# Padding the rows of the moving operands, and eight start residues for the weight slots

## What is computed

```
x = x + 0.5 * swiglu(rmsnorm(x, ffn1_norm[l]), w_ffn1_in[l], w_ffn1_out[l])
u = rmsnorm(x, mix_norm[l])
... = split_sizes(u @ w_in[l], IN_SPLITS)
...
x = x + merged @ w_out[l]
x = x + 0.5 * swiglu(rmsnorm(x, ffn2_norm[l]), w_ffn2_in[l], w_ffn2_out[l])
```

## Time and profile before

| | |
|---|---|
| time, median of 3 runs | 2471.56 us |
| time of the profiled execution | 2470.84 us |
| span of the profiled execution | 2469.0 us |
| TensorE matmul busy | 2440.9 us (99%), 20,948 matmul records |
| TensorE weight load busy | 2380.7 us (96%) |
| VectorE busy | 1673.3 us (68%) |
| ScalarE busy | 1279.0 us (52%) |
| GpSimd busy | 404.8 us (16%) |
| moved by DMA | 410.11 MB, mean 166 GB/s |
| granted TensorE clock, mean | 0.996 of full speed |

### The profile page before, as it was taken

The page is one execution under the profiler, slowest core; times in us unless marked ns, Lnnn a source line. Parts: engine busy times, 40 slices in busy tenths (PEclk is TensorE's granted clock), DMA queues, the critical chain, the costliest instruction groups (busy, mean ns, idle before and its releaser), DMA issues.

```text
span 2469.0 us, 49272 instructions
## 1 busy us (share of the span) xinstructions
PE 2440.9 (99%) x20948; PEld 2380.7 (96%) x20948; DVE 1673.3 (68%) x2315; ACT 1279.0 (52%) x1812; POOL 404.8 (16%) x357
## 2 busy tenths in 40 slices
PE   8999999999999999999999999999999999999998
PEld 8999999999999999999999999989999999999998
DVE  7765776866667657878666766866666665866664
ACT  5544656644445456565454544745444444754443
POOL 4012110300200210203003013512002003422001
PEclk9999999999999999999999999999999999999999
DMA  6555433455555544345555555403555555402553
GB/s 241 188 188 180 162 124 133 173 188 186 188 188 188 188 171 154 120 139 195 185 190 191 205 203 183 155 19 120 186 185 179 187 189 186 161 26 98 193 188 120
DMA packets 57675, 410.11 MB, mean 166 GB/s; under 512 B 6384, under 2 KB 6640, under 8 KB 8688
## 3 DMA queue, kind: packets, MB, share of 16 engines
q1 hardware_dynamic: 56592, 402.15, 45.9%
q10 hardware_dynamic: 864, 4.82, 0.5%
HBM read 405.89 MB, written 1.05 MB: 165 GB/s over the span
## 4 chain that ended last, share of the span: by engine, by line
PE 87%; DVE 5%; ACT 3%; issue 3%; POOL 2%; DMA 0%; DVEq 0%; SPq 0%; POOLq 0%; ACTq 0%
PE bank L297 86%; DVE sb_wlo L310 2%; ACT area L306 2%; DVE area L310 2%; DVE area L321 1%; PE bank L301 1%; ACT sb_whi L306 1%; POOL area L310 0%; ACT L306 0%; POOL sb_x_ssq L310 0%; POOL area L315 0%; POOL sb_x_sq L310 0%; DVE sb_x L321 0%; DMA sb_x<-x 0%; POOL area L334 0%
## 5 line engine op out<-in xcount | busy, mean ns | idle before, releaser
L297 PE MATMUL bank<-area,sb_whi 128*128 128x256 f32 x11752 | 2093.6, 281 | 11.0 <-DVE area L321 5.7
L297 PEld LDWEIGHTS bank<-area,sb_whi 128*128 128x128 f32 x11752 | 1799.7, 188 | 23.8 <-DVE area L321 9.6
L297 PE MATMUL bank<-area,sb_wlo 128*128 128x256 f32 x5876 | 1642.3, 279 | 4.5 <-DVE sb_wlo L310 4.4
L306 ACT ACTIVATE sb_whi<-sb_raw 128x1024 fp32r<-128x1024 f32 x762 | 801.9, 1058 | 777.0 <-PE bank L297 771.0
L297 PEld LDWEIGHTS bank<-area,sb_wlo 128*128 128x128 f32 x5876 | 1103.6, 188 | 6.4 <-DVE sb_wlo L310 6.4
L310 DVE TENSOR_TENSOR sb_wlo<-sb_raw,sb_whi 128x1024 fp32r<-128x1024 f32 x762 | 962.0, 1271 | 163.2 <-ACT sb_whi L306 161.8
L310 DVE TENSOR_TENSOR area<-area,area 128x256 f32<-128x256 f32 (+7 forms) x502 | 259.7, 526 | 248.4 <-ACT area L306 245.7
L306 ACT ACTIVATE area<-area 128x256 f32<-128x256 f32 (+6 forms) x515 | 252.1, 498 | 83.9 <-DVE area L310 59.1
L310 DVE TENSOR_TENSOR area<-bank,sb_x_diag 128x512 f32<-128x512 f32 x244 | 167.3, 686 | 36.2 <-PE bank L297 21.6
L297 PE MATMUL bank<-area,area 128*64 128x64 f32 (+5 forms) x2304 | 181.4, 254 | 2.1 <-ACT area L306 1.9
L310 POOL TENSOR_TENSOR sb_x_ssq<-sb_x 128x256 f32<-128x256 f32 x12 | 13.1, 1088 | 1014.9 <-DVE sb_x L321 883.0
(11 more groups left out here) (82 smaller groups left out, 705.7 us busy)
## 6 DMA issues: line engine op xcount, KB each, us to landing
sb_raw<-stream SPq DMA_DIRECT2D x379, 1024.0 KB, 4.8
sb_raw<-stream SPq DMA_DIRECT2D x4, 512.0 KB, 6.9
area<-lora ACTq DMA_DIRECT2D x2, 768.0 KB, 4.5
area<-c ACTq DMA_DIRECT2D x1, 1504.0 KB, 7.2
sb_x<-x SPq DMA_DIRECT2D x4, 256.0 KB, 5.0
area<-mem ACTq DMA_DIRECT2D x1, 1024.0 KB, 8.2
out<-sb_x SPq DMA_DIRECT2D x4, 256.0 KB, 2.9
area<-m ACTq DMA_DIRECT2D x1, 512.0 KB, 5.8
```

Of the source, the lines that this page charges most:

```text
L297: return lambda e: e.matmul(out, lhsT, rhs, start=start, stop=stop, skip_group_check=True, tile_position=at)
L306: return lambda e: e.activation(out, a, f, **kw)
```

## The change

No instruction is added, removed or moved. On every engine the program issues the same instructions in the same order; what differs is at which byte of a partition their operands lie.

- `xh` and `xl` rows are `XT = T + 8` elements apart (1056 bytes, 32 more than before), of which the first 256 are used. The eight `xh` rows then start at 0, 32, ..., 224 bytes past a multiple of 512, and the eight `xl` rows at 256, 288, ..., 480.
- The arena starts at a multiple of 1024. All other rows in it (`hh`, `hl`, the mixer's) stay 1024 bytes apart without padding, so they all start at a multiple of 1024.
- The eight weight slots get different residues of 512: `whi` slots 0 to 3 at 0, 128, 256 and 384; `wlo` slots 0 to 3 at 64, 192, 320 and 448. All blocks of one slot share its residue.
- The raw slots move, and the scratch for DMA descriptors shrinks to 1024 bytes to make room.

```diff
+ROW = 4 * T
+RESIDUES = ((0, 0, 0), (1, 0, 64), (0, 1, 128), (1, 1, 192), (0, 2, 256), (1, 2, 320), (0, 3, 384), (1, 3, 448))
...
-ARENA = (XH + 16) * T
+XT = T + 8
+ARENA = XH * T + 16 * XT
...
+def place(k, end):
+    k.arena = (end - 4 * ARENA) // ROW * ROW
+    at, k.split_at = k.arena, {}
+    for part, i, rest in RESIDUES[::-1]:
+        at = (at - 4 * PIECE * 128 - rest) // ROW * ROW + rest
+        k.split_at[part, i] = at
+    k.raw_at = []
+    for i in range(RAW_SLOTS):
+        at -= 4 * CHUNK_BLOCKS * 128
+        k.raw_at.append(at // 32 * 32)
+    return k.raw_at[-1]
...
-    w.raw = [sbuf(k, f"raw{i}", [128, CHUNK_BLOCKS * 128]) for i in range(RAW_SLOTS)]
-    w.hi = [sbuf(k, f"whi{i}", [128, PIECE * 128], F32R) for i in range(SPLIT_SLOTS)]
-    w.lo = [sbuf(k, f"wlo{i}", [128, PIECE * 128], F32R) for i in range(SPLIT_SLOTS)]
+    nc, piece, chunk = k.nc, [128, PIECE * 128], [128, CHUNK_BLOCKS * 128]
+    w.hi, w.lo = ([nc.alloc_sbuf_tensor_at(f"sb_{name}{i}", piece, F32R, offset=k.split_at[part, i])
+                   for i in range(SPLIT_SLOTS)] for part, name in enumerate(("whi", "wlo")))
+    w.raw = [nc.alloc_sbuf_tensor_at(f"sb_raw{i}", chunk, F32, offset=k.raw_at[i]) for i in range(RAW_SLOTS)]
...
-        k.xh, k.xl = (area(k, (XH + NX * i) * T, NX, T, dt=F32R) for i in range(2))
+        k.xh, k.xl = (area(k, XH * T + NX * XT * i, NX, XT, dt=F32R)[:, :, 0:T] for i in range(2))
...
-    nc = bacc.Bacc("TRN2", target_bir_lowering=False, num_devices=1)
+    nc = bacc.Bacc("TRN2", target_bir_lowering=False, num_devices=1, dynamic_dma_scratch_size=1024)
```

More of the change, by code:

```diff
@@ L2589, in program @@
         k.sx, k.scratch = scales(k, "x"), sbuf(k, "scratch", [128, 2])[:, :]
-        ctx.enter_context(nc.sbuf_tensor("arena", [128, ARENA], F32, side="right"))
-        k.arena, k.placed = nc.sbuf_usable_end // 32 * 32 - 4 * ARENA, 0
-        k.xh, k.xl = (area(k, (XH + NX * i) * T, NX, T, dt=F32R) for i in range(2))
+        k.placed = 0
+        low = place(k, nc.sbuf_usable_end // 32 * 32)
+        ctx.enter_context(nc.sbuf_tensor("placed", [128, (nc.sbuf_usable_end - low) // 32 * 8], F32, side="right"))
+        k.xh, k.xl = (area(k, XH * T + NX * XT * i, NX, XT, dt=F32R)[:, :, 0:T] for i in range(2))
         k.x_done, k.xh_done, k.xl_done = [0] * NX, [0] * NX, [0] * NX
```

## The result

The changed kernel takes 2480.59 us (median of 5 runs, 2479.38 to 2482.16), the kernel before 2471.77 us (5 runs, 2469.4 to 2474.74). The ratio is 1.0037, with a 95% interval from 1.0025 to 1.0049: slower by 0.4%, where 1.9% faster was forecast.

What follows compares the result with a forecast made beforehand. TensorE's matmul spacing was taken to bound the kernel. Only `xh` and `xl` matmuls gain, 47.4 us, all else 0 us: 2471.6 - 47.4 = 2424 us, with an 8 in 10 range of 2390 to 2482 us.

Steps and rivals of the forecast that it cites:

- What bounds the kernel: TensorE holds 87% of the chain; its 17,628 matmuls cost their spacing, with only 11.0 + 4.5 us idle ahead of them.
- Two paces, kept once chosen, without a part of the clock, DMA or the other engines: Feed-forward matmuls run at 0.1177 or 0.1133 us each, changing only at interruptions, whatever clock, DMA, VectorE and ScalarE do.
- Raw slots, smaller scratch, the addresses that ScalarE and VectorE write: Moved raw slots, less DMA scratch and new ScalarE and VectorE write addresses: 0 us, as TensorE doesn't wait for them.
- Where it changes at every matmul, the pattern can't repeat itself, while the faster pace, in which nothing is delayed, has no reason to end: Changing row-to-weight distances give `xh` and `xl` matmuls the faster pace: (11,712 - 1030) x 4.44 ns = 47.4 us gained.
- never the same one twice running: For the 11,712 matmuls on `xh` and `xl`, the row-to-weight distance takes 16 values equally often and differs every time.
- the other rows ... at the slower: The 5916 matmuls on `hh`, `hl` and mixer rows, whose distance still repeats, stay at 0.1177 us: no gain.
- from both sides by the two paces that exist: The cost per matmul lies between 0.1133 and 0.1177 us, and beyond them by estimate only.
- the slower one: Rival, chance 0.22: changing distances lose the fast stretch, 7 us (2479 us), and worse distances add 39 us (2518 us).
- No change: Rival, chance 0.28: addresses have no part in the matmul spacing; 2471.6 us, between 2467 and 2476.
- all rows gain: Rival: all 16,070 slow matmuls gain 4.44 ns each, 71 us, to 2400 us; faster in either degree had 0.50.
- The Trainium skill: Moving operand and weight load have a read port each, so by it alone the change gives 0 us, 2471.6 us.
- The estimate of 109.2 ns: An undisturbed 256-column matmul takes 256 / 2.4 + 2.5 = 109.2 ns; a full gain would be 145 us.

Runs made afterwards that it cites:

- distance 320: Changed kernel without padding, all slots at residue 192, one constant distance as in the kernel before: 2478.94 us, ratio 1.0028 to the kernel before.
- 192: Changed kernel without padding, all slots at residue 320, constant distance of 192 modulo 512: 2421.71 us, ratio 0.9804 to the kernel before.
- 448: Changed kernel without padding, all slots at residue 64, constant distance of 448 modulo 512: 2434.12 us, ratio 0.9836 to the kernel before.
- 416: Changed kernel without padding, all slots at residue 96, constant distance of 416 modulo 512: 2488.43 us, ratio 1.0067 to the kernel before.

## Why the prediction was wrong

- *What bounds the kernel*: right. Spacing, not waits, is what moved, in every kernel of the study.
- *Two paces, kept once chosen, without a part of the clock, DMA or the other engines*: right. The windows of all kernels keep their pace at a granted clock of 1.00 and addresses alone move it.
- *Raw slots, smaller scratch, the addresses that ScalarE and VectorE write*: 0 us, right within what was measured: the kernel at distance 320 has the same moves and keeps the pace of 117.7 ns; its 7.2 us over before are the lost fast feed-forward.
- *"Where it changes at every matmul, the pattern can't repeat itself, while the faster pace, in which nothing is delayed, has no reason to end"*: this is the step that failed. Instead of the 113.3 ns that it gave to `xh` and `xl`, they run at 118.4. The padding alone gives them 118.5 too, where the same slots without padding (distance 320) give 117.7, so it is the changing distance that does it. Repeating is not what makes a pace slow: held constant, distances give levels from 113.2 to 120.0 ns, and only 64 and 192 modulo 256 have the fast one at all. Not only is nothing gained, but the long fast stretch ends. Why a mix gives the level it does stays open. The premise was off as well: "never the same one twice running" is true modulo 512. Modulo 256 there are 8 values, not 16, and the first two matmuls of each block, `wh` by `xh` and `wh` by `xl`, have the same one.
- *"the other rows ... at the slower"*: wrong by 0.96 ns, in the kernel's favour. With the distances of eight slots, four values modulo 256, they come out at 116.8 ns.
- *The bounds "from both sides by the two paces that exist"*: too narrow. Distances that the trace of before didn't hold are up to 2.3 ns slower. The one other distance in it misled: `gemm_rows` at 192 was at the slower pace, and in `gemm` 192 is the best of all.
- *The rivals*: the slower one named the mechanism: the end of the fast stretch (7 us, measured 7.2) and worse distances among the sixteen. It was priced at 0.22 and is what happened, with the rest of its price (39 us) cancelled down to 2.1 us. The time lies 1.4 us inside the range, whose end was set for the lost fast stretch. That it came so near to the 2479 us of that rival is partly luck: two terms that nobody had forecast, 7.3 us lost and 5.2 us gained, nearly cancel. *No change* fell with 448 and 192, and *all rows gain* got 0.96 of its 4.44 ns, on the other rows only.
- *The Trainium skill*, "SBUF — State Buffer", section "Who interferes with whom", by which nothing could change: the measurements disagree. With the same instructions and only other addresses of TensorE's two operands the time runs from 2421.7 to 2513.4 us, so the spacing depends on the two addresses together, which independent ports don't explain, and the measurement decides. The estimate of 109.2 ns takes the formula in the Trainium skill's "TensorE: Matmul & The Clock Gate", section "Back-to-back issue gap", which is given there for an isolated matmul and not for a stream with weight loads. No run shows this spacing; the best is 113.2.

The evidence that would have helped was missing from the trace, not overlooked: it held one distance only in `gemm`. But one experiment of that kind, the distance set to another constant value, would have shown more than the change did.

## What to carry to other kernels

If matmuls follow one another without waits and still stand further apart than their columns explain, change the distance between the moving and the stationary operand's start (here in steps of 32 bytes, modulo 256) and measure each value held constant. Spreading them doesn't get the best: the two mixes here ran at 118.4 and 116.8 ns, the best constant distance at 113.2. Look at the spacing stretch by stretch, not at its mean: two paces in one kernel show that there is something to win. A fast stretch that exists by luck is a part of the time before, and a shift of addresses can lose it, as at distance 320. It also pays to look at every execution of the kernel before: a step of 7 us between them is nearly the size of the whole effect of this change.

## What the runs showed of the hardware

The spacing of 256-column float32r matmuls, each with a new weight load, isn't a fixed cost: with one distance held, at a granted clock of 1.00, it was 113.2, 116.6, 117.3, 117.7, 118.3, 118.6 or 120.0 ns (each to 0.1), by the operands' distance modulo 256 bytes as far as tested, and stayed so for up to 1558 matmuls. The same distance has up to three such levels (416 shows three), and the pace changed only where the stream was interrupted. That rows and slots moved together by 96 bytes leave the levels but take the fast one from seven of eight feed-forwards was not expected, and its cause stays open.
